# A two-layer hybrid decoder on one core: norms by block and half, router tables spread over an expert, and products that nothing reads at norms and router

## What is computed

```python
def reference(x, ...):
    for layer in range(DEPTH):                       # DEPTH = 2
        h = rms_norm(x, norm_mix[layer])
        x = x + hybrid_mixer(h, w_in[layer], ...)    # 4 branches, gates, one output projection
        h = rms_norm(x, norm_ffn[layer])
        if layer % 2 == 0:
            x = x + swiglu(h, w_gate, w_up, w_down)  # dense, hidden width 2816
        else:
            x = x + moe_swiglu(h, router, ...)       # top 2 of 8 experts, hidden width 3584
    return rms_norm(x, final_norm)

def rms_norm(x, g):
    y = x * rsqrt(mean(x * x, axis=-1) + 1e-6)
    return y * g
```

## Time and profile before

| what | value |
| --- | --- |
| three runs | 1862.64 us median (1860.69 to 1862.9) |
| the profiled execution's own time | 1863.15 us |
| its span (first to last instruction) | 1860.9 us |
| PE busy | 1770.2 us (95%), 10378 matmuls |
| DVE busy | 1496.2 us (80%) |
| ACT busy | 1128.3 us (61%) |
| granted PE clock, mean | 0.978 of full speed |
| HBM traffic | 267 GB/s over the span |

### The profile page before, as it was taken

How to read it: one execution, slowest core, us unless ns; L and a number is a source line. 1 busy time by engine, 2 the same in 40 slices (tenths; PEclk the granted TensorE clock), 3 DMA queues, 4 the chain that set the end, 5 groups by cost and what they waited for, 6 DMA issues and landing times.

```text
span 1860.9 us, 27428 instructions
## 1 busy us (share of the span) xinstructions
PE 1770.2 (95%) x10378; PEld 1556.5 (84%) x10378; DVE 1496.2 (80%) x1475; ACT 1128.3 (61%) x911; POOL 58.1 (3%) x48
## 2 busy tenths in 40 slices
PE   6999999899989999995999999999999999999996
PEld 6999888799979998884788888888888888888885
DVE  3999976544449999766688889889898898888986
ACT  3456554433334564543577777777777777777774
POOL 0000000000000000000000000000000000000000
PEclk9999999999989999996899999999999999999999
DMA  6454444655344543435699999999999999999993
GB/s 245 149 169 159 136 131 144 243 181 186 122 138 137 170 150 135 130 128 228 250 373 368 386 386 362 405 364 381 390 360 403 371 377 392 370 392 372 375 407 129
DMA packets 237503, 497.57 MB, mean 267 GB/s; under 512 B 19296, under 2 KB 43872, under 8 KB 237296
## 3 DMA queue, kind: packets, MB, share of 16 engines
q1 hardware_dynamic: 233104, 479.65, 70.9%
q0 software_dynamic: 4320, 16.82, 2.8%
HBM read 488.55 MB, written 7.86 MB: 267 GB/s over the span
## 4 chain that ended last, share of the span: by engine, by line
PE 82%; DVE 13%; ACT 2%; DMA 2%; issue 1%; SPq 0%; DVEq 0%; ACTq 0%
PE pair L892 57%; PE aux L892 20%; DVE lo_ring L1395 4%; PE pair L1313 1%; DMA raw_ring<-in_w_in 1%; DVE arena L1583 1%; DVE arena L1569 1%; ACT hi_ring L505 1%; DVE small L1582 1%; DMA raw_ring<-in_mg 0%; DMA raw_ring<-in_fu 0%; PE aux L1132 0%; DVE pair L1541 0%; DVE mrg L1548 0%; PE aux L905 0%
## 5 line engine op out<-in xcount | busy, mean ns | idle before, releaser
L1395 DVE TENSOR_TENSOR lo_ring<-raw_ring,hi_ring 128x2048 fp32r<-128x2048 f32 x276 | 623.0, 2262 | 133.5 <-ACT hi_ring L505 132.0
L505 ACT ACTIVATE hi_ring<-raw_ring 128x2048 fp32r<-128x2048 f32 x276 | 522.4, 1894 | 285.6 <-PE pair L892 196.5
L1395 DVE TENSOR_TENSOR lo_ring<-arena,hi_ring 128x2048 fp32r<-128x2048 f32 x183 | 418.3, 2289 | 79.5 <-ACT hi_ring L505 79.5
L505 ACT ACTIVATE hi_ring<-arena 128x2048 fp32r<-128x2048 f32 x183 | 350.3, 1919 | 136.7 <-PE pair L892 80.2
L892 PE MATMUL pair<-hT_lo,hi_ring 128*128 128x256 f32 (+1 forms) x1360 | 392.8, 289 | 19.2 <-DVE hT_lo L1415 8.7
L892 PE MATMUL pair<-hT_hi,lo_ring 128*128 128x256 f32 (+1 forms) x1360 | 388.4, 286 | 0.0
L892 PE MATMUL pair<-hT_hi,hi_ring 128*128 128x256 f32 (+1 forms) x1360 | 388.2, 285 | 0.0
L892 PE MATMUL pair<-lo_ring,hT_hi 128*128 128x512 f32 x896 | 356.6, 398 | 9.2 <-DVE hT_lo L1911 6.8
L892 PE MATMUL pair<-hi_ring,hT_hi 128*128 128x512 f32 x896 | 351.1, 392 | 0.0
L892 PE MATMUL pair<-hi_ring,hT_lo 128*128 128x512 f32 x896 | 350.6, 391 | 0.0
L892 PEld LDWEIGHTS pair<-hT_lo,hi_ring 128*128 128x128 f32 (+1 forms) x1360 | 263.5, 194 | 27.3 <-DVE hT_lo L1415 9.7
(11 more groups left out here) (311 smaller groups left out, 1792.3 us busy)
## 6 DMA issues: line engine op xcount, KB each, us to landing
raw_ring<-in_mu SPq DMA_DIRECT2D x222, 512.0 KB, 5.8
arena<-in_mg SPq DMA_DIRECT2D x220, 512.0 KB, 5.8
raw_ring<-in_w_in SPq DMA_DIRECT2D x120, 512.0 KB, 4.4
arena<-in_md SPq DMA_DIRECT2D x114, 512.0 KB, 5.0
raw_ring<-in_md SPq DMA_DIRECT2D x110, 512.0 KB
raw_ring<-in_w_br SPq DMA_DIRECT2D x32, 512.0 KB, 4.5
raw_ring<-in_w_out SPq DMA_DIRECT2D x16, 512.0 KB, 4.6
raw_ring<-in_fg SPq DMA_DIRECT2D x12, 512.0 KB, 6.7
```

The lines of the kernel that those rows point to most:

```text
L505: nc.scalar.activation(hi_ring[:, h, 0:cols], raw(slot)[:, 0:cols], ACT.Copy).then_inc(hi_ready, 1)
L1395: nc.vector.tensor_tensor(lo_ring[:, h, 0:cols], raw(slot)[:, 0:cols], hi_ring[:, h, 0:cols].bitcast(f32), ALU.subtract).then_inc(lo_ready, 1)
```

## The change

It rewrites five parts.

1. **Norms by block and half.** x is summed, squared and scaled in pieces of 512 columns; each piece has its own semaphore count. `NORM_ORDER` says in which order the four pieces (block, half) of a norm come. The two out-blocks of the last product and three of the four parts of the last dense product signal apart (`out_block`, `dense_part`). The second panel of the next stage is converted behind `norm_hi` and `norm_lo` and not ahead of them. In norm 0, x comes in two transfers, the first gain goes to SP's queue ahead of the weights, and POOL issues parameters and constants only when x is normed; ACT converts one panel, not two, ahead of `norm_hi`.
2. **Router and tables.** hi and lo of the router are one tile of 16 columns, so two products for each k-tile do; DVE adds the halves. After `make_pick(0)` DVE goes to `hx_lo`. The sums for extra slots are one pass over all three (`extra_slots`), inside step 0; the tables come in groups of 8 in steps 0, 1 and 2, `index_slots` and `places` in step 3.
3. **Tail.** The last expert's result is split, scattered, added and squared by halves, the final norm by block.
4. **Four moves** in the mixer: `gated` writes its product over the gate in `arena` and frees the pair; `branch_lo(1)` stands behind the panel conversion; the root's table is loaded by `warm_sqrt` behind the square; the last branch is split by halves.
5. **Products that nothing reads** (`keep`): PE multiplies the identity by itself, 128x512, into `pair0`: 5 + 2 + 4 around the transposes of norms 1 and 2, 5 + 2 + 8 in norm 3, and 10, 6 and 10 around the counts and the gather.

```diff
             def norm(n):
+                square(n, 2)
+                root(n, 0)
+                square(n, 3)
+                root(n, 1)
+
+            def square(n, i):
+                b, half = NORM_ORDER[n][i]
+                if n == 0:
+                    act.wait_ge(*((S["x_in1"], 16) if b else (x_in, 16)))
+                else:
+                    act.wait_ge(S["x_summed"], 4 * (n - 1) + i + 1)
+                nc.scalar.activation(hN[:, b, half * 512:(half + 1) * 512], x[:, b, half * 512:(half + 1) * 512], ACT.Square,
+                                     accum_out=small[:, 2 * b + half:2 * b + half + 1]).then_inc(S["squared"], 1)
+
+            def root(n, b):
+                act.wait_ge(S["meaned"], 2 * n + b + 1)
+                nc.scalar.activation(small[:, 8 + b:9 + b], small[:, 4 + b:5 + b], ACT.Sqrt).then_inc(S["rooted"], 1)
+
...
                     act.wait_ge(S["one_set"], 1)
                 warm_sqrt()
-                for b in range(NB):
-                    if n == 0 and b == 0:
-                        act.wait_ge(x_in, 16)
-                    if n and b == 0:
-                        act.wait_ge(*{1: ev(0, "out1"), 2: (S["dense_added"], 1), 3: ev(1, "out1")}[n])
-                    nc.scalar.activation(hN[:, b, :], x[:, b, :], ACT.Square,
-                                         accum_out=small[:, b:b + 1]).then_inc(S["squared"], 1)
-                act.wait_ge(S["meaned"], n + 1)
-                nc.scalar.activation(small[:, 4:6], small[:, 2:4], ACT.Sqrt).then_inc(S["rooted"], 1)
...
+                warm_sqrt()
...
-                act.wait_ge(S["branch_f"], L + 1)
-                branch_hi(3)
-                gate("g3h1", "br1h1")
+                for h in range(2):
+                    act.wait_ge(S["branch_f"], 2 * L + h + 1)
+                    nc.scalar.activation(act_hi[:, 1024 + h * 512:1536 + h * 512], ar(A_UPAD + h * 512, 512), ACT.Copy)\
+                       .then_inc(S["branch_hi"] if h else S["last_hi"], 1)
+                gate("g3h1", 4)
...
+            act.wait_ge(S["half_down"], 1)
+            output_hi(0)
+            act.wait_ge(panel_used, EXP_BASE + exp_at(exp_end, 1) + 1)
+            output_hi(1)
```

```diff
+            def keep(count):
+
+                for _ in range(count):
+                    pe.matmul(pairs[CH_INDEX["out0"] % 2][:, 0:512], ident_r[:, :],
+                              ident_r[:, :].unsqueeze(1).broadcast_to([128, 4, 128]), start=True, stop=True)
+
             def norm(n):
                 if n == 0:
                     pe.wait_ge(ident_in, 16)
+                elif n % 2:
+                    pe.wait_ge(S["x_summed"], 4 * (n - 1) + 2)
                 for b in range(NB):
-                    pe.wait_ge(S["normed"], 2 * n + b + 1)
+                    if n:
+                        keep((5, 2)[b])
                     for k in range(KT):
+                        if k % 4 == 0:
+                            pe.wait_ge(S["normed"], 4 * n + 2 * b + k // 4 + 1)
                         ins = pe.transpose(aux[:, k * T + b * 128:k * T + (b + 1) * 128], hN[:, b, k * 128:(k + 1) * 128],
                                            C("ident"))
                         if b == NB - 1 and k % 2:
                             ins.then_inc(S["turned"], 1)
+                if n:
+                    keep(8 if n == 3 else 4)
...
+                for n, r in enumerate((hT_lo, hT_hi)):
+                    ins = pe.matmul(aux[0:16, 1024:1280], rt[:, k, :], r[:, k, :], start=(k == 0 and n == 0),
+                                    stop=(k == KT - 1 and n == 1))
             ins.then_inc(S["routed_T"], 1)
...
+            keep(10)
             pe.wait_ge(S["masks_done"], 1)
...
+                keep(6)
                 pe.wait_ge(S["pick_done"], 1)
...
+                keep(10)
...
+                    if s == 3 and first:
                         index_slots()
```

```diff
+            def norm_mean(n, b):
+                dve.wait_ge(S["squared"], 4 * n + NORM_ORDER[n].index((b, 1)) + 1)
+                link(nc.vector.tensor_scalar(small[:, 4 + b:5 + b], small[:, 2 * b:2 * b + 1], 1.0 / D, EPS, ALU.mult, ALU.add))
+                nc.vector.scalar_tensor_tensor(small[:, 4 + b:5 + b], small[:, 2 * b + 1:2 * b + 2], 1.0 / D, small[:, 4 + b:5 + b],
+                                               ALU.mult, ALU.add).then_inc(S["meaned"], 1)
+
+            def norm_scale(n, b, between=lambda: None):
+                dve.wait_ge(S["rooted"], 2 * n + b + 1)
+                link(nc.vector.reciprocal(small[:, 14 + b:15 + b], small[:, 8 + b:9 + b]))
+                dve.wait_ge(*((gain_in, 16 * n) if n else (S["first_gain"], 16)))
+                for half in range(2):
+                    if half:
+                        between()
+                    c = slice(half * 512, (half + 1) * 512)
+                    nc.vector.scalar_tensor_tensor(hN[:, b, c], x[:, b, c], small[:, 14 + b:15 + b], gain[:, c], ALU.mult,
+                                                   ALU.mult).then_inc(S["normed"], 1)
+
+            def norm(n, last=lambda: None):
+                norm_mean(n, 0)
+                last()
+                norm_scale(n, 0, lambda: norm_mean(n, 1))
+                norm_scale(n, 1)
...
+                    gates = ar(A_GATES + h * 1024, 1024)
+                    nc.vector.tensor_tensor(gates, g[:, :], gates, ALU.mult).then_inc(emptied["D"], 1)
 
                 def add_gated(i, h):
-                    g = pair_of(f"br{BR_ORDER[i]}h{h}")
                     dst = mrg[:, h * 1024:(h + 1) * 1024]
-                    dve.wait_ge(S["branch_gated"], 6 * L + 2 * i + h - 1)
-                    nc.vector.tensor_tensor(dst, g[:, :], dst, ALU.add).then_inc(emptied["D"], 1)
+                    dve.wait_ge(*ev(L, f"br{BR_ORDER[i]}h{h}"))
+                    nc.vector.tensor_tensor(dst, ar(A_GATES + h * 1024, 1024), dst, ALU.add).then_inc(S["branch_added"], 1)
...
                 topk_mask(0)
+                lo_upto(CH_PANEL["g0h1"] + 2)
                 branch_lo(1)
-                lo_upto(CH_PANEL["g0h1"] + 2)
...
+                def add_out(h, b):
                     name = f"out{h}"
-                    dve.wait_ge(panel_used, used_after(L, name))
-                    xs = x[:, :, h * 512:(h + 1) * 512]
-                    nc.vector.tensor_tensor(xs, pair_of(name)[:, :].rearrange("p (b n) -> p b n", b=NB), xs, ALU.add)\
-                      .then_inc(emptied["D"], 1)
+                    if h == 0 and b == 0 or h == 1 and b == 1:
+                        dve.wait_ge(panel_used, used_after(L, name))
+                    elif h == 1:
+                        dve.wait_ge(S["out_block"], L + 1)
...
+                    nc.vector.tensor_tensor(xs, pair_of(name)[:, b * 512:(b + 1) * 512], xs, ALU.add).then_inc(S["x_summed"], 1)
+
+                add_out(0, 0)
+                add_out(0, 1)
+                base = EXP_BASE if L else DENSE_BASE
+                to_lo(base, 0, PANEL, base % HRING)
+                if L:
+                    split_router()
+                add_out(1, 0)
+                norm(2 * L + 1, lambda: add_out(1, 1))
+                norm_lo(2 * L + 1)
+                to_lo(base + 1, 1, PANEL, (base + 1) % HRING)
 
```

```diff
+                    for b in range(NB):
+                        nc.vector.tensor_scalar(ar(A_PICKS + (c * NB + b) * 128, 128), C("iota"), pos_t[:, b, c:c + 1], None,
+                                                ALU.is_equal).then_inc(S["picks_done"], 1)
...
                         exp_lo(n, 1)
+                    else:
+                        count_full()
...
+                    else:
+                        extra_slots()
                     exp_hid(n)
-                    if s == 0 and first:
+                    if s < 3 and first:
+                        some_picks(4 * s, 4 * s + 4)
+                    if s == 2 and first:
+                        tokens()
+                    if s == 3 and first:
                         places()
```

And on SP and POOL at the start:

```diff
+            sp.dma_start(x[:, 0, :], x_d[0:128, :]).then_inc(x_in, 16)
+            sp.dma_start(x[:, 1, :], x_d[128:256, :]).then_inc(S["x_in1"], 16)
+            sp.dma_start(gain[:, :], gains_d[0:1, :].broadcast_to([128, D])).then_inc(S["first_gain"], 16)
...
+                    pool.wait_ge(S["normed"], 4 * n)
+                    pool.dma_start(gain[:, :], gains_d[n:n + 1, :].broadcast_to([128, D])).then_inc(gain_in, 16)
                 if n == 0:
+                    pool.wait_ge(S["normed"], 4)
```

289 lines of the change are left out of this document (157 added, 132 removed).

## The result

The changed kernel takes 1830.45 us (median of 4 runs, 1824.79 to 1831.24) against 1861.66 us before (median of 4, 1860.38 to 1862.9). The ratio is 0.9826, 95% interval 0.9804 to 0.9848: 31 us faster, where 45 were forecast, and 1.5 us above the upper end of the range. The profiled execution took 1831.24 us with a span of 1829.1, so the two profiles differ by 31.8 us in span.

A forecast was written before the change was run, and what follows sets the result against it. PE, busy 95% of the span, was taken as the bound, leaving its waits and the half clock behind them to win. Terms summed to 44.9: 1863.15 - 44.9 = 1818.2 us; range 1806 to 1829 (all bounds 1805 to 1842).

The forecast's parts named there:

- Opening, -6.6: Start of layer 0: first panel lands near 9.7 us, PE starts near 15.15 instead of 21.78; gain between 3 and 8.
- Attention part, -1.1 each: Attention part of both mixers: freed pair and kept clock give -1.7, late state-space input costs 0.7; from -3.8 to +2.
- The stall on DVE: Both mixers: ACT's panel conversion waits for the later `branch_lo`, losing DVE 1.95 us; as a rival 1824 us, chance 0.07.
- Last branch, -3.8 each: Last branch of both mixers: table load 1.1 and halves 1.0 off the path, slow panel 1.7; from 0 to -4.5.
- Norm 1, -5.5: Out product to dense product, layer 0: PE's gap of 10.9 us becomes 5.4 by working in pieces; from 4 to 6.5.
- Tail, -4.0: Last expert's result to the end: work by halves, last piece scaled 3.4 us earlier, last transfer 0.6 less; 2.5 to 5.5.
- Norm 2, -7.0: Between the stages before layer 1: gap 11.3 to 6.6 us (-4.7), slow start of layer 1 goes (-2.3); 3 to 7.5.
- Norm 3, router, first expert, -12: Norm 3 gives 4.7, pick at 863.2, first expert begins at 870.4 instead of 882.42; from 6.5 to 15.
- clock regained by the time of the gather: Router: at full clock the gather takes 3.6 us instead of 7.1; at half clock PE begins at 874 to 875.
- the first rival: Clock falls all the same at norm 2 (loses 2.3) and router with gather (4.5): 1825 us; chance 0.17.
- The first expert therefore takes as long as before: First expert: moved tables and `index_slots` add no time overall, less the slow clock at its start (48 products 13.50 against 10.91).
- they just fit: Tables, 1.6 us on DVE in each of steps 0 to 2; a full step is 16.8 us, DVE busy for 14.9.

## Why the prediction failed

- **Opening, -6.6; measured -5.3.** The mechanism held. The first panel was converted at 11.28, not near 9.7: by then 3.2 MB had moved, since the next panels' transfers share the queues from the start. Alone in the queues it still came only 0.5 us earlier, so the rest of the 1.6 is the rate. Nor was norm 0 done near 9.7, as I had it: the gain landed at 8.69 and DVE scaled until 11.89. Sized 1.3 too high.
- **Attention part, -1.1 each; measured -0.9 each.** The stall on DVE cost the 2 us worked out, and the freed pair gave 2.05 back and the clock behind it. What I had not seen is that the stall brings PE a wait of its own, 1.98 us for L1716, with a clock fall behind it. That fall cost nothing by itself: in the experiment with the filled waits the clock happened to hold there in layer 1, and the 1.5 us so won were waited away before the freed pair was reached. The wait was cheap to avoid: the experiment gained 2.05 us in each mixer by undoing that one move.
- **Last branch, -3.8 each; measured -2.4 and about -2.4.** (Layer 1's 3.3 of the table holds 0.9 of the attention part.) The clock held, and gave 1.4 to 1.5. The wait only shrank from 2.2 to 1.16 us, 1.0 instead of 2.1. PE then waits for something I didn't count, the gate read by ACT out of the pair that PE has just filled itself. The profile names no releaser, but the program has `free` wait for just this reader, and PE starts 0.1 us behind its end:

```profile
283.99 1.03 ACT L574 ACTIVATE arena<-pair 128x1024 f32<-128x1024 f32 x1 [0.71 <-PE pair L925]
...
285.12 0.35 PE L925 MATMUL pair<-act_lo,hi_ring 128*128 128x256 f32 x1 [1.16 <-issue]
```

- **Norm 1, -5.5; measured -5.1. Tail, -4.0; measured -4.2.** Right in size; PE's gap at norm 1 went from 10.9 to 5.9 us, 5.4 forecast.
- **Norm 2, -7.0; measured -5.5.** "PE stands still for 1.5 us at most, and the slow start of layer 1 goes": it stood still for 1.38 us at one piece, and the slow start did go, worth 2.1 us of the 2.3. What fell short is the gap, 11.4 to 7.8 us where 6.6 was forecast: the 3.4 us at half clock lay inside it, from 516.4 on, over transposes and unread products, and cost 1.0 us. With 11 products ahead of block 0 instead of 5 it went; it also went in two executions with 5.
- **Norm 3, router, first expert, -12; measured -5.0. This is the step that failed**, in two places. First, "clock regained by the time of the gather": it wasn't. The gather took 6.7 us and not 3.6, `hx_lo` came at 849.06, 2.4 us later than I took, and the ten unread products behind the gather stuck out by another 1.2; the first expert product came 8.3 us earlier and not 12. This was the first rival (the clock falls all the same at norm 2 and router), given 0.17. Ten unread products fill 2.1 of the 4.8 us that PE waits for the masks without any; filling the wait won the gather's 3.2 us at once. Second, "The first expert therefore takes as long as before" (the 12 counts its start alone, and its slow first panel was to go besides): from its first product to the last down product of step 3 it took 74.5 us instead of 71.2. The wait in step 0 was forecast (3.4 us, measured 3.1), and the kernel before has one of 2.37 at the same place, with half clock around it:

```profile
904.51 0.79 PE L892 MATMUL pair<-lo_ring,hT_hi 128*128 128x512 f32 x1 [2.37 <-DVE lo_ring L1395]
```

  What I had at nothing is the clock behind `index_slots`. In step 0 before, a part of the half clock behind those 48 products passed while PE waited anyway; in step 3 full down products stand there, and they lost 2.8 us. By the two timelines the changed kernel wins 2.4 us in the first panel and 4.6 where `index_slots` stood, and loses 0.6 at the step-0 wait, 1.1 in waits of steps 1 and 2 ("they just fit": nearly), 5.8 for `index_slots` in step 3 and 2.8 for the clock behind it: 3.3 lost in all.
- The tables in step 0 could have been free. DVE's work there is not spread over the step, it is a chain (hidden product, tables, conversion, next product), and what stands in a chain counts in full, whatever the engine's share: put ahead of the hidden product, the 1.65 us of tables took 1.57 off PE's wait.
- The range was too narrow because I treated the falls of the clock as one rival with one price; between the opening and the end the changed kernel has six of them, at five kinds of place. The bounds of the terms as written also add up to 1804 to 1848 us, not 1805 to 1842.
- The two rules of the Trainium skill. "ScalarE: Activation LUTs" (What ACT_TABLE_LOAD costs), about 2.66 us for a switch with its drain: the trace before shows 1.28 us for the load and the root 0.02 us behind it, without a drain, so the measurement decides; the term missed for another reason. "TensorE: Matmul & The Clock Gate" (Part 4), transposes don't count as busy: the trace agrees at norm 2, where the clock fell among the 16 transposes, and does not decide it, since at norm 1 it held without any unread product. Its case, that the clock falls all the same, came true at norm 2 and the router with the products in place, since they did not fill the waits.

## What to carry to other kernels

Fill a wait of TensorE whole or leave it: 10 products in a wait of 4.8 us bought little there, 22 won the stage behind it. Before moving small work off an engine's path, look for where that engine stands still, and put it there; inside a steady loop, a share of busy time under 100% doesn't say that there is room, the chain does. A long run of very small products was followed by half clock as a pause is; here it paid to split it up.

## What was not expected of the hardware

Whether the granted clock falls behind a wait of 1.4 to 2.6 us differs between executions: norm 2's wait of 1.38 us was followed by 3.4 us at 1.2 GHz in one kernel and the same wait of 1.39 us by none in another. An experiment that shifts the work by a few us can therefore also change what the clock does at every later place, some 4 us at the router here, and a difference of medians must be read with the granted clock beside it. Still, over the 13 profiled executions from the changed kernel on, the waits decide most of it. With 22 products at the masks the clock held from there through the gather in all six executions; with 10 it fell in all five, and was down through the whole gather in two; with none it fell in both. At norm 2 it held in all six with 11 products, in two of five with 5, in neither without. And 48 products of 3 columns, during which PE counts as fully busy for 5.8 us, were followed in step 3 by 3.4 or 6.8 us at 1.2 GHz in all nine profiled executions that have them there; as three groups of 16 with full products between them they were followed by none, in both executions.
